# Gates and down projection of a SwiGLU MLP in three chunks of 6, 8 and 8 gates in place of four of 6, 6, 5 and 5

## The chip, the cores and the metric

The kernel runs on one core of a Trainium2 chip, in one launch. The metric is device time in microseconds (us), lower is better.

## The reference, cut to what matters

Two transformer layers over 128 context tokens and 512 latent tokens. The part that matters here is the end of each layer, the MLP, with D_MODEL = 1024 and D_FF = 2816:

```python
h2 = _rmsnorm(x, norm2_g[l]) * (1 + sc2) + sh2
a, b = jnp.split(_dwconv3(h2 @ w_up[l], ffn_conv_w[l]), 2, axis=-1)
x = x + g2 * ((jax.nn.silu(a) * b) @ w_down[l])
```

`_dwconv3` is a depthwise convolution of width 3 along the tokens. Everything is float32.

## The kernel before

**Tiling.** Tokens lie along the free dimension, T = 644 columns (640 tokens and the borders), in two halves of 322. Features lie on the 128 partitions. The 2816 hidden features are 22 gates of 128 (`N_GATE`); gate g needs a 128-column block of the a side and one of the b side of `w_up`. For float32 results each operand is split into a high part (a copy to float32r) and a low part (the difference), and every product is three matmuls: high x high, high x low, low x high. ScalarE makes the high parts of weights, VectorE the low parts.

**Gates.** Gates 0 and 6 (`CLASSIC`) are computed with plain products ahead of the loop. Each of the other 20 is computed by Strassen's scheme in seven products of 12 matmuls (128x128 by 128x322; `product`, L1185, L1187, L1189), with weights that are sums of blocks of `w_up`. SP loads seven blocks of 256 KB a gate (`up_blocks`, `block`, L565) into `raw_all`, an area of nine blocks of 512 columns; POOL makes three of the sums with adding DMAs from SBUF to SBUF (`add_block`, L678) and one with an instruction (L708). ScalarE then copies block pairs 0, 1 and 2 and last the single block A22 to `w_hi` (`up_split_hi`, L1638, L1625), and VectorE writes `w_lo` (`up_split_lo`, L2235, L2231). VectorE and ScalarE combine the seven products (L1656, L2250, L2258, L2267, L1582), apply the convolution (L1596, L2196) and silu (L1601), multiply (L2217) and split the result into `gg`, the gates' results of a chunk (L1611, L2223). `gg` holds as many gates as the largest chunk.

**Down projection.** After each chunk of gates, `down_chunk` multiplies its gates with their rows of `w_down`: 8 output tiles m, each of two token halves, each of 3 matmuls per gate (L1242, L1243, L1244) into two PSUM banks. The first two tiles leave out their last gate until it is ready. VectorE adds each tile to x (`down_add`, L2130, three pieces a tile). The weights come in four quarters of two tiles (`down_block`, L622), 256 columns a gate, alternately into slot 0 and slot 1 of `raw_all` (blocks 0 to 3 and blocks 4 to 7), and are split by L1649 and L2242. A quarter of a chunk of 5 or 6 gates is 1280 or 1536 columns, and leaves block 7 of slot 1 free.

**Order.** All queues are written out by hand, each engine's program in one order, with waits on semaphores. For the first gate of a chunk SP issues A22 (block 7) and the block for the first sum (block 8) right after the third quarter of the down weights of the chunk before; blocks 0, 2 and 3 after the third quarter's low part; blocks 4 and 5 after the fourth quarter's (`dn_lo[1]`):

```python
elif i == 0:
    sp.wait_ge(up_lo[3], n)
block(a22_block(g), 1, 1, g)
```

For the first quarter of the down weights ScalarE waits until the third product of the last gate is done. After the last layer, ten transposes of x (L820) go to PSUM banks by the list `YT_BANKS`, the first three ahead of the last down tile.

Of the kernel before, what the change touches and what calls it, by code (L numbers as in the profile page):

```python
# [8 lines left out]
F32R = mybir.dt.float32r  # L9
# [6 lines left out]
P = 128  # L16
# [13 lines left out]
T = 644  # L30
# [23 lines left out]
N_GATE = FF // P  # L54
CLASSIC = [0, 6]
N_CLASSIC = len(CLASSIC)
CHUNKS = [6, 6, 5, 5]
CH0 = [0, 6, 12, 17]
S_LAYER = N_GATE - N_CLASSIC
FIRST = 1  # L60
HELD = CLASSIC[1]
# [57 lines left out]
def chunk_of(g):  # L119

    return max(c for c in range(len(CHUNKS)) if CH0[c] <= g)


def s_gates(c):

    return [g for g in range(CH0[c], CH0[c] + CHUNKS[c]) if g not in CLASSIC]

# [14 lines left out]
def a22_block(g):  # L142

    return 7 - (g - s_gates(chunk_of(g))[0]) % 2


def s1_block(g):

    return (8, 1)[(g - s_gates(chunk_of(g))[0]) % 2]
# [5 lines left out]
def su(l, g):  # L155

    return S_LAYER * l + S_GATES.index(g)
# [15 lines left out]
def dm(l, c, m):  # L173

    return 8 * (len(CHUNKS) * l + c) + m


def dq(l, c, q):

    return 2 * (len(CHUNKS) * l + c) + q // 2  # L180

# [6 lines left out]
N_SMALL = 8  # L188
N_ROWS = 10

YT_BANKS = [6, 7, 0, 1, 3, 4, 2, 5, 6, 7]
YT_EARLY = 3
YT_WAITS = {0: 4, 2: 6, 4: 7, NT: KT}
OT_BANKS = [2, 3, 4, 0, 1]
# [17 lines left out]
def hybrid_step(nc, x_prompt, x_sample, cache_k, cache_v, c_sample, c_ctx, w_mod, b_mod, norm1_g, w_in, q_norm_g,  # L212
# [3 lines left out]
    with ctx:  # L216
        def sb(name, shape, dt=F32, scope=None):
            return (scope or ctx).enter_context(nc.sbuf_tensor(name, shape, dt))

        def sem(name):  # L220
            return ctx.enter_context(nc.semaphore(name))
# [81 lines left out]
        mlp = ExitStack()  # L303
# [18 lines left out]
        g_early = sb("g_early", [P, 2, 2, T], scope=plain)  # L322
        hfull = sb("hfull", [P, KT, T], scope=plain)
        plain.close()
        gg = sb("gg", [P, CHUNKS[0], 2, T], F32R, scope=mlp)
        mlp.close()
        ps = ctx.enter_context(nc.psum_tensor("ps", [P, 8, 512], F32))
        scores = ps[:, 2:5, :].rearrange("p b n -> p (b n)")
# [59 lines left out]
        dn_full, dn_hi, dn_lo = ([sem("%s%d" % (s, i)) for i in range(2)] for s in ("dn_full", "dn_hi", "dn_lo"))  # L388
        prod_done, gate_read = sem("prod_done"), sem("gate_read")
# [35 lines left out]
        def _(sp):  # L425
# [44 lines left out]
            for l in range(DEPTH):  # L470
                def free_of_split(n):
                    sp.wait_ge(split_full[n % 2], usable(l, n))
# [5 lines left out]
                def split_unit(n):  # L478
                    if n < C_U + 6:
                        if n < C_U:  # L480
                            load(n % 2, w_in_v, l * KT + n % 2 * KH, KH, n // 2 * QC, QC)
                        else:
                            pair, kind = divmod(n - C_U, 3)
                            col = 3 * D_ATTN + D_CONV * (1, 2, 0)[kind] + pair * UC
                            load(n % 2, w_in_v, l * KT, KT, col, UC)
                    else:
                        load(n % 2, w_out_v, l * KT, KT, (n - O_U) * UC, UC)
# [47 lines left out]
                if l:  # L535
                    sp.wait_ge(dn_lo[1], dq(l - 1, len(CHUNKS) - 1, 3) + 1)
                    split_unit(1)
# [21 lines left out]
                def free_of_slot0():  # L559

                    free_of_split(G_U)

                def block(b, row, half, g):

                    sp.dma_start(raw_f[:, BLK * b:BLK * (b + 1)].rearrange("p (t n) -> p t n", n=P),  # L565
                                 w_up_v[:, l * KT + KH * half:l * KT + KH * (half + 1),
                                        row * FF + g * P:row * FF + (g + 1) * P]).then_inc(blk_full[b], 16)

                def up_blocks(g):

                    n, c = su(l, g), chunk_of(g)
                    i = g - s_gates(c)[0]
                    if i >= 2:
                        sp.wait_ge(up_lo[3], n - 1)
                    elif c == 0:
                        free_of_split(G_U + 1)
                    elif i == 0:
                        sp.wait_ge(up_lo[3], n)
                    block(a22_block(g), 1, 1, g)
                    if i >= 2:  # L580
                        sp.wait_ge(up_lo[0], n - 1)
                        sp.wait_ge(sum_full[2], 16 * (n - 1))
                    elif i == 0 and n:
                        sp.wait_ge(up_lo[0], n)
                        sp.wait_ge(sum_full[2], 16 * n)
                    elif c == 0 and i:
                        free_of_slot0()
                    block(s1_block(g), 1, 0, g)
                    if i:
                        sp.wait_ge(up_lo[0], n)  # L590
                        sp.wait_ge(sum_full[4], 16 * n)
                    elif c == 0:
                        free_of_slot0()
                    else:
                        sp.wait_ge(dn_lo[0], dq(l, c - 1, 2) + 1)
                    block(0, 0, 0, g)
                    if i:
                        sp.wait_ge(up_lo[1], n)
                        sp.wait_ge(sum5_ready, n)
                    block(2, 0, 0, g)  # L600
                    block(3, 0, 1, g)
                    if i:
                        sp.wait_ge(up_lo[2], n)
                    elif c:
                        sp.wait_ge(dn_lo[1], dq(l, c - 1, 3) + 1)
                    block(4, 1, 0, g)
                    block(5, 0, 1, g)

                def down_block(c, q):
# [9 lines left out]
                    else:  # L619
                        sp.wait_ge(dn_lo[q % 2], dq(l, c, q - 2) + 1)  # L620
                    k0 = l * (FF // P) + CH0[c]
                    sp.dma_start(raw[:, q % 2, 0:CHUNKS[c] * DW].rearrange("p (t n) -> p t n", n=DW),  # L622
                                 w_down_v[:, k0:k0 + CHUNKS[c], q * DW:(q + 1) * DW]).then_inc(dn_full[q % 2], 16)

                for c in range(len(CHUNKS)):
                    for g in s_gates(c):
                        up_blocks(g)
                    for q in range(4):
                        down_block(c, q)
# [100 lines left out]
        def _(pe):  # L730
# [81 lines left out]
            def turn_out(j):  # L812
# [6 lines left out]
                for s in range(4):  # L819
                    ins = nc.tensor.transpose(ps[:, YT_BANKS[j], s * P:(s + 1) * P],  # L820
                                              x[:, 4 * kh + s, TOK_TILES[t]:TOK_TILES[t] + P], ident[:, :])
# [57 lines left out]
            for l in range(DEPTH):  # L879
# [353 lines left out]
                def down(c, m, k0, k1):  # L1233

                    kf, b = CHUNKS[c], m // 2 % 2
                    wh, wl = (half[:, b, 0:kf * DW].rearrange("p (t n) -> p t n", n=DW)[
                        :, :, m % 2 * P:(m % 2 + 1) * P] for half in (w_hi, w_lo))
                    for h in range(2):
                        out = ps[:, down_banks(c, m)[h], 0:HALF]
                        for k in range(k0, k1):  # L1240
                            gh, gl = (gg[:, k, i, h * HALF:(h + 1) * HALF] for i in range(2))
                            mm(out, wh[:, k, :], gh, start=k == 0, stop=False)  # L1242
                            mm(out, wh[:, k, :], gl, start=False, stop=False)  # L1243
                            ins = mm(out, wl[:, k, :], gh, start=False, stop=k == kf - 1)  # L1244
                    if k1 == kf:
                        ins.then_inc(dn_done, 1)

                def down_chunk(c):

                    kf, n = CHUNKS[c], su(l, s_gates(c)[-1])  # L1250
                    pe.wait_ge(dn_lo[0], dq(l, c, 0) + 1)
                    pe.wait_ge(g_ready, N_GATE * l + CH0[c] + kf - 1)
                    pe.wait_ge(c21_ready, n)
# [3 lines left out]
                    down(c, 1, 0, kf - 1)  # L1257
                    pe.wait_ge(g_ready, N_GATE * l + CH0[c] + kf)
                    down(c, 0, kf - 1, kf)
# [27 lines left out]
        def _(act):  # L1287
# [74 lines left out]
            for l in range(DEPTH):  # L1362
# [240 lines left out]
                def gate_hi(g):  # L1603
# [5 lines left out]
                    if g == FIRST + 1:  # L1609
                        act.wait_ge(t_ready, 4 * l + 4)  # L1610
                    A(gg[:, g - CH0[c], 0, :], gt[:, :], ACT.Copy).then_inc(gh_ready, 1)  # L1611

# [27 lines left out]
                def down_split_hi(c, q):  # L1640

                    n = su(l, s_gates(c)[-1])
                    if q < 2:
                        act.wait_ge(prod_done, 7 * n + (3, 7)[q])
                    else:
                        act.wait_ge(dn_done, dm(l, c, 2 * q - 3) + 1)
                    act.wait_ge(dn_full[q % 2], 16 * (dq(l, c, q) + 1))
                    w = CHUNKS[c] * DW
                    A(w_hi[:, q % 2, 0:w], raw[:, q % 2, 0:w], ACT.Copy).then_inc(dn_hi[q % 2], 1)  # L1649
# [17 lines left out]
                for c in range(len(CHUNKS)):  # L1667
# [31 lines left out]
                    c21(last)  # L1699
                    centre(last, 1)  # L1700
                    down_split_hi(c, 1)
                    silu(last)
                    gate_hi(last)
                    if last + 1 == HELD:
                        centre(HELD, 0)
                        centre(HELD, 1)
                    down_split_hi(c, 2)
                    if last + 1 == HELD:
                        silu(HELD)
# [18 lines left out]
            for j in range(2 * NT):  # L1728
                act.wait_ge(yT_full, j + 1)
                kh, t = divmod(j, NT)  # L1730
                A(yo[:, t, kh * 512:(kh + 1) * 512], ps[:, YT_BANKS[j], :], ACT.Copy).then_inc(yT_read, 1)

# [673 lines left out]
```

## Time and profile before

| | |
|---|---|
| median of 3 runs | 1567.98 us (1566.52 to 1570.54) |
| the profiled execution's own time | 1567.95 us |
| its span, first to last instruction | 1566.1 us |
| mean granted TensorE clock | 0.995 |
| TensorE busy | 1549.9 us, 99% |
| VectorE busy | 1046.8 us, 67% |
| ScalarE busy | 726.9 us, 46% |
| POOL busy | 188.3 us, 12% |

The page and the trace are of one execution. Busy time is the union of an engine's instructions over the span; what is outside the span lies ahead of the first instruction and behind the last. In the rows below PE is TensorE, DVE VectorE, ACT ScalarE, SP the queue that issues most DMAs; a letter q behind an engine means its sequencer. Matmuls overlap in the pipeline: one takes 310 ns and starts about 150 ns after the one before it. The MLP of layer 0 lies from about 358 to 797 us, that of layer 1 from about 1118 to 1558 us.

### The profile page before, as it was taken

The numbers are of one execution on the slowest core, as the hardware profiler recorded it, in microseconds if no ns is written. First come the engines' busy times: TensorE is split into PE (matmuls) and PEld (weight loads), VectorE is DVE, ScalarE is ACT, GpSimd is POOL, SyncE is SP. The second block draws the span as 40 slices with busy tenths as digits, with TensorE's granted clock in tenths as the row PEclk, the third lists the DMA queues.
The fourth block names the chain that finished last, engine by engine and source line by source line (L and its number), as shares of the span: only waits on it lengthen the run. The fifth ranks groups of instructions, "written<-read, shape, count | busy, mean of one in ns | idle before, by whom it ended". The sixth has DMA issues, their size and how long they took to land.

```text
span 1566.1 us, 26388 instructions
## 1 busy us (share of the span) xinstructions
PE 1549.9 (99%) x10573; PEld 1456.5 (93%) x10573; DVE 1046.8 (67%) x1661; ACT 726.9 (46%) x1218; POOL 188.3 (12%) x197
## 2 busy tenths in 40 slices
PE   8999999999999999999999999999999999999998
PEld 6778899998999999999987788899899999999998
DVE  6763767738785855858777447685688677486683
ACT  5444444326652634626454344542565355263462
POOL 1000000004202202113000000000221120130210
PEclk9999999999999999999999999999999999999999
DMA  9653011475756846659453501033367584584752
GB/s 361 244 174 136 28 54 37 156 240 138 179 142 141 199 127 160 163 146 201 155 183 127 202 28 55 28 109 108 95 145 165 137 186 132 149 192 134 181 140 85
DMA packets 278366, 225.63 MB, mean 144 GB/s; under 512 B 9674, under 2 KB 253700, under 8 KB 278244
## 3 DMA queue, kind: packets, MB, share of 16 engines
q1 hardware_dynamic: 259680, 189.89, 38.1%
q0 software_dynamic: 18320, 33.96, 12.8%
q8 instruction: 84, 1.38, 0.4%
q14 instruction: 38, 0.31, 0.1%
q10 hardware_dynamic: 244, 0.09, 0.0%
HBM read 188.78 MB, written 3.67 MB: 123 GB/s over the span
## 4 chain that ended last, share of the span: by engine, by line
PE 96%; DVE 2%; DMA 1%; ACT 1%; SPq 0%; issue 0%; DVEq 0%; ACTq 0%
PE ps L1185 11%; PE ps L1187 11%; PE ps L1189 11%; PE ps L1242 7%; PE ps L1244 7%; PE ps L1243 7%; PE ps L739 4%; PE ps L740 4%; PE ps L741 4%; PE ps L894 4%; PE ps L895 3%; PE ps L896 3%; PE ps L1034 3%; PE ps L1061 3%; PE ps L1101 3%; PE ps L1102 2%
## 5 line engine op out<-in xcount | busy, mean ns | idle before, releaser
L1638 ACT ACTIVATE w_hi<-raw_all 128x1024 fp32r<-128x1024 f32 x120 | 126.3, 1058 | 203.1 <-PE ps L1244 100.0
L1242 PE MATMUL ps<-gg,w_hi 128*128 128x322 f32 x704 | 218.5, 310 | 0.0
L1244 PE MATMUL ps<-gg,w_lo 128*128 128x322 f32 x704 | 218.2, 310 | 0.0
L1243 PE MATMUL ps<-gg,w_hi 128*128 128x322 f32 x704 | 218.1, 310 | 0.0
L1187 PE MATMUL ps<-hc_lo,w_hi 128*128 128x322 f32 x640 | 199.5, 312 | 0.0
L1185 PE MATMUL ps<-hc_hi,w_hi 128*128 128x322 f32 x640 | 199.0, 311 | 0.0
L1189 PE MATMUL ps<-hc_hi,w_lo 128*128 128x322 f32 x640 | 198.6, 310 | 0.0
L2235 DVE TENSOR_TENSOR w_lo<-raw_all,w_hi 128x1024 fp32r<-128x1024 f32 x120 | 147.7, 1230 | 72.4 <-ACT w_hi L1638 70.2
L678 POOL DMA_DIRECT2D raw_all<-raw_all x120 | 102.6, 860 | 552.6 <-DMA raw_all<-in_w_up_dram 481.0
L2196 DVE SCALAR_TENSOR_TENSOR tmp<-ub,vecs,tmp 128x642 f32<-128x642 f32 x168 | 140.9, 883 | 15.2 <-ACT tmp L1596 13.7
L2130 DVE SCALAR_TENSOR_TENSOR x<-ps,modv,x 128x128 f32<-128x128 f32 (+2 forms) x240 | 90.4, 434 | 89.8 <-PE ps L1244 54.3
L1185 PE MATMUL ps<-ht_hi,w_hi 128*128 128x322 f32 x480 | 148.8, 310 | 0.0
L1189 PE MATMUL ps<-ht_hi,w_lo 128*128 128x322 f32 x480 | 148.5, 309 | 0.0
L1187 PE MATMUL ps<-ht_lo,w_hi 128*128 128x322 f32 x480 | 148.1, 308 | 0.0
L1242 PEld LDWEIGHTS ps<-gg,w_hi 128*128 128x128 f32 x704 | 132.6, 188 | 0.0
L1244 PEld LDWEIGHTS ps<-gg,w_lo 128*128 128x128 f32 x704 | 132.6, 188 | 0.0
L1243 PEld LDWEIGHTS ps<-gg,w_hi 128*128 128x128 f32 x704 | 132.4, 188 | 0.0
L739 PE MATMUL ps<-h_hi,w_hi 128*128 128x322 f32 x384 | 123.6, 322 | 0.0
L1185 PEld LDWEIGHTS ps<-hc_hi,w_hi 128*128 128x128 f32 x640 | 120.7, 189 | 0.0
L1187 PEld LDWEIGHTS ps<-hc_lo,w_hi 128*128 128x128 f32 x640 | 120.6, 188 | 0.0
L1189 PEld LDWEIGHTS ps<-hc_hi,w_lo 128*128 128x128 f32 x640 | 120.6, 188 | 0.0
L1821 DVE TENSOR_TENSOR w_lo<-raw_all,w_hi 128x2048 fp32r<-128x2048 f32 x33 | 75.5, 2288 | 66.7 <-ACT w_hi L1346 66.7
(236 smaller groups left out, 3549.0 us busy)
## 6 DMA issues: line engine op xcount, KB each, us to landing
raw_all<-in_w_up_dram SPq DMA_DIRECT2D x280, 256.0 KB, 4.0
raw_all<-raw_all POOLq DMA_DIRECT2D x120, 256.0 KB, 3.9
raw_all<-in_w_in_dram SPq DMA_DIRECT2D x48, 512.0 KB, 6.9
mod_p<-in_w_mod_dram SPq DMA_DIRECT2D x20, 1024.0 KB, 7.3
raw_all<-in_w_down_dram SPq DMA_DIRECT2D x16, 768.0 KB, 4.4
raw_all<-in_w_down_dram SPq DMA_DIRECT2D x16, 640.0 KB, 4.1
mod_q<-in_w_mod_dram SPq DMA_DIRECT2D x8, 1024.0 KB, 9.2
raw_all<-in_w_out_dram SPq DMA_DIRECT2D x16, 512.0 KB, 4.3
```

The costliest lines, as they stand in the source:

```text
L678: pool.dma_start(raw_f[:, BLK * dst:BLK * (dst + 1)], raw_f[:, BLK * src:BLK * (src + 1)], accum_op=ALU.add).then_inc(sum_full[which], 16)
L739: mm(out, wh[:, k, col:col + P], mov_hi(k), start=k == 0, stop=False)
L1185: mm(out, whi_f[:, c0:c0 + P], hh[:, k, slot, :], start=first and k == 0, stop=False, skip_group_check=not first)
L1187: mm(out, whi_f[:, c0:c0 + P], hl[:, k, slot, :], start=False, stop=False, skip_group_check=not first)
L1189: ins = mm(out, wlo_f[:, c0:c0 + P], hh[:, k, slot, :], start=False, stop=k == KH - 1, skip_group_check=not first)
L1242: mm(out, wh[:, k, :], gh, start=k == 0, stop=False)
L1243: mm(out, wh[:, k, :], gl, start=False, stop=False)
L1244: ins = mm(out, wl[:, k, :], gh, start=False, stop=k == kf - 1)
L1638: A(whi_b[:, 2 * i:2 * (i + 1), :], src, ACT.Copy).then_inc(up_hi[i], 1)
L2130: ins = V.scalar_tensor_tensor(out=xs, in0=ps[:, banks[h], p0:p0 + n], scalar=gate, in1=xs, op0=ALU.mult, op1=ALU.add)
L2196: return V.scalar_tensor_tensor(out=cen[:, s, 1:T - 1], in0=u[:, s, j:j + T - 2], scalar=vecs[:, l, w:w + 1], in1=cen[:, s, 1:T - 1], op0= ...
L2235: V.tensor_tensor(wlo_b[:, pair, :], raw_b[:, pair, :] if i else first_pair(g), whi_b[:, pair, :].bitcast(F32), ALU.subtract).then_inc(up_ ...
```

## The change

The 22 gates of a layer are cut into chunks of 6, 8 and 8 in place of 6, 6, 5 and 5, so there are three passes of the down projection a layer in place of four. `gg` gets room for 8 gates. Quarters of the down weights of a chunk of 8 are 2048 columns and fill their slot. So the first gate of a later chunk fetches A22, and with it all that stands behind it in SP's queue, after the low part of the fourth quarter of the chunk before; and ScalarE's first copy of down weights waits for the fourth product of the last gate, since it overwrites one more block. The banks of the last transposes change with the parity of the banks of the last chunk. The room that POOL's DMAs have for descriptors is set to 2048 bytes of a partition.

```diff
@@ -54,8 +54,8 @@
 N_GATE = FF // P
 CLASSIC = [0, 6]
 N_CLASSIC = len(CLASSIC)
-CHUNKS = [6, 6, 5, 5]
-CH0 = [0, 6, 12, 17]
+CHUNKS = [6, 8, 8]
+CH0 = [0, 6, 14]
 S_LAYER = N_GATE - N_CLASSIC
 FIRST = 1
 HELD = CLASSIC[1]
@@ -188,7 +188,7 @@
 N_SMALL = 8
 N_ROWS = 10
 
-YT_BANKS = [6, 7, 0, 1, 3, 4, 2, 5, 6, 7]
+YT_BANKS = [6, 7, 3, 4, 0, 1, 2, 5, 6, 7]
 YT_EARLY = 3
 YT_WAITS = {0: 4, 2: 6, 4: 7, NT: KT}
 OT_BANKS = [2, 3, 4, 0, 1]
@@ -322,7 +322,7 @@
         g_early = sb("g_early", [P, 2, 2, T], scope=plain)
         hfull = sb("hfull", [P, KT, T], scope=plain)
         plain.close()
-        gg = sb("gg", [P, CHUNKS[0], 2, T], F32R, scope=mlp)
+        gg = sb("gg", [P, max(CHUNKS), 2, T], F32R, scope=mlp)
         mlp.close()
         ps = ctx.enter_context(nc.psum_tensor("ps", [P, 8, 512], F32))
         scores = ps[:, 2:5, :].rearrange("p b n -> p (b n)")
@@ -576,6 +576,7 @@
                         free_of_split(G_U + 1)
                     elif i == 0:
                         sp.wait_ge(up_lo[3], n)
+                        sp.wait_ge(dn_lo[1], dq(l, c - 1, 3) + 1)
                     block(a22_block(g), 1, 1, g)
                     if i >= 2:
                         sp.wait_ge(up_lo[0], n - 1)
@@ -1641,7 +1642,7 @@
 
                     n = su(l, s_gates(c)[-1])
                     if q < 2:
-                        act.wait_ge(prod_done, 7 * n + (3, 7)[q])
+                        act.wait_ge(prod_done, 7 * n + (4, 7)[q])
                     else:
                         act.wait_ge(dn_done, dm(l, c, 2 * q - 3) + 1)
                     act.wait_ge(dn_full[q % 2], 16 * (dq(l, c, q) + 1))
@@ -2391,7 +2392,8 @@
     import concourse.bacc as _bacc
     from concourse.bass_utils import run_bass_kernel_spmd as _run
 
-    nc = _bacc.Bacc("TRN2", target_bir_lowering=False, num_devices=1)
+    nc = _bacc.Bacc("TRN2", target_bir_lowering=False, num_devices=1,
+                     dynamic_dma_scratch_size=2048)
     tables = _tables()
     arrays, args = {}, []
     for name in _INS + ["ident", "rope"]:
```

## Rows read from the trace of the kernel before

Each group is of the one profiled execution.

**Rows 1.** The page: busy time of the engines, the chain, costly groups

```profile
PE 1549.9 (99%) x10573; PEld 1456.5 (93%) x10573; DVE 1046.8 (67%) x1661; ACT 726.9 (46%) x1218; POOL 188.3 (12%) x197
...
PE 96%; DVE 2%; DMA 1%; ACT 1%; SPq 0%; issue 0%; DVEq 0%; ACTq 0%
...
L1242 PE MATMUL ps<-gg,w_hi 128*128 128x322 f32 x704 | 218.5, 310 | 0.0
...
L2130 DVE SCALAR_TENSOR_TENSOR x<-ps,modv,x 128x128 f32<-128x128 f32 (+2 forms) x240 | 90.4, 434 | 89.8 <-PE ps L1244 54.3
...
L1821 DVE TENSOR_TENSOR w_lo<-raw_all,w_hi 128x2048 fp32r<-128x2048 f32 x33 | 75.5, 2288 | 66.7 <-ACT w_hi L1346 66.7
```

**Rows 2.** Waits of TensorE: waited for, us in total, times, longest

```profile
PE ps L1159 <- DVE hc_lo L2179: 3.1, 2, 2.0
...
PE ps L894 <- DVE h_lo L1909: 0.3, 1, 0.3
```

**Rows 3.** Busy time by stretch: four gates, down chunks of 6 and 5

```profile
391.90:441.80 49.90, 49.90 (x340) 49.90 (x339) 40.07 (x50) 34.31 (x51) 14.16 (x14) 1.00 0.75 176
454.20:496.80 42.60, 42.60 (x290) 42.60 (x289) 24.00 (x37) 11.43 (x13) 5.59 (x6) 1.00 0.55 141
...
663.70:699.20 35.50, 35.50 (x243) 35.50 (x242) 19.25 (x32) 8.49 (x9) 5.55 (x6) 1.00 0.58 155
```

**Rows 4.** TensorE in order of time, both ends of a down chunk

```profile
454.07 0.31 PE L1189 MATMUL ps<-hc_hi,w_lo 128*128 128x322 f32 x1
454.22 0.31 PE L1242 MATMUL ps<-gg,w_hi 128*128 128x322 f32 x1
...
496.80 0.31 PE L1185 MATMUL ps<-hc_hi,w_hi 128*128 128x322 f32 x1
```

**Rows 5.** ScalarE, then VectorE in order of time, ahead of that chunk

```profile
448.28 1.48 ACT L1649 ACTIVATE w_hi<-raw_all 128x1536 fp32r<-128x1536 f32 x1
...
449.10 0.49 DVE L2250 TENSOR_TENSOR ub<-ps,s 128x322 f32<-128x322 f32 x1 [1.63 <-PE ps L1189]
...
451.27 1.75 DVE L2242 TENSOR_TENSOR w_lo<-raw_all,w_hi 128x1536 fp32r<-128x1536 f32 x1
```

**Rows 6.** ScalarE's groups by form

```profile
L1346 ACT ACTIVATE w_hi<-raw_all 128x2048 fp32r<-128x2048 f32 x35 | 66.9, 1913 | 8.6 <-PE ps L896 8.6
```

**Rows 7.** SP, VectorE, POOL in order of time, during that chunk

```profile
440.79 22.13 SPq L622 DMA_DIRECT2D raw_all<-in_w_down_dram  x4
462.96 57.37 SPq L565 DMA_DIRECT2D raw_all<-in_w_up_dram  x25
...
479.02 2.02 SPq L565 DMA_DIRECT2D raw_all<-in_w_up_dram  x4
...
477.23 1.76 DVE L2242 TENSOR_TENSOR w_lo<-raw_all,w_hi 128x1536 fp32r<-128x1536 f32 x1 [4.25 <-ACT w_hi L1649]
...
482.37 0.84 POOL L678 DMA_DIRECT2D raw_all<-raw_all  x1 [6.32 <-DMA raw_all<-in_w_up_dram]
```

**Rows 8.** ScalarE, then VectorE in order of time, for gate 8

```profile
504.11 1.06 ACT L1638 ACTIVATE w_hi<-raw_all 128x1024 fp32r<-128x1024 f32 x1 [0.71 <-PE ps L1189]
...
506.29 1.22 DVE L2235 TENSOR_TENSOR w_lo<-raw_all,w_hi 128x1024 fp32r<-128x1024 f32 x1
```

**Rows 9.** DMAs issued at L565, L678 and L622, in this order

```profile
DMA to landing us min/median/max: 2.7/4.0/6.8
...
DMA to landing us min/median/max: 3.1/3.9/6.9
...
DMA to landing us min/median/max: 4.0/4.3/5.6
```

**Rows 10.** What L1185 waited for; ScalarE in order of time before it

```profile
  ACT s L1656: 0.3, 1
...
1189.76 1.06 ACT L1638 ACTIVATE w_hi<-raw_all 128x1024 fp32r<-128x1024 f32 x1 [3.12 <-DMA raw_all<-raw_all]
```

**Rows 11.** POOL in order of time, around its 113th DMA

```profile
1350.95 0.86 POOL L678 DMA_DIRECT2D raw_all<-raw_all  x1 [1.17 <-DMA raw_all<-in_w_up_dram]
```

## The prediction

> **What bounds the kernel now.** I read first the page's busy shares and its chain. TensorE is busy 1549.9 of 1566.1 us and holds 96% of the chain that ended last [rows 1]. A busy share can still hide stalls, so I read next TensorE's own waits: ten entries, 12 us together, the longest 3.1 us before the MLP's first matmuls, and none at a line of the gates or the down projection [rows 2]; only the view of L1185 by itself shows one of 0.3 us there [rows 10]. Third, the stretches that the change touches. TensorE is busy in every one of the 49.90 us of four gates and of the 42.60 and 35.50 us of a down chunk of 6 and one of 5, at a granted clock of 1.00 [rows 3]. Fourth, the seams: from gates to down projection one matmul starts 0.15 us after the other, as everywhere else, and at the way back, 496.80, the busy stretch of 42.60 us ends without a hole [rows 3, 4]. So the seams that the change takes away (one each way in each layer, four in all) cost TensorE nothing today.
>
> **TensorE's sum.** The down projection has the same matmuls: 22 gates x 8 tiles x 2 halves x 3 x 2 layers = 2112, which is 3 x 704 [rows 1]. A chunk of 6 takes 42.60 us, so 5.33 us for each of its 8 tiles; one of 5 takes 35.5, 4.44 a tile [rows 3]. One of 8 should take 42.60 x 8/6 = 56.8, 7.10 a tile. Per layer that is 2 x 42.6 + 2 x 35.5 = 156.2 us before and 42.6 + 2 x 56.8 = 156.2 after. The gates' 40 x 84 matmuls stay as well. TensorE's term is 0, and what is left is whether one of its waits turns up.
>
> **What is removed.** One pass a layer that adds the down result to x: 8 tiles x 3 pieces x 2 layers = 48 of VectorE's instructions at 434 ns [rows 1], 20.8 us. They lie beside TensorE's gapless stream, so they are worth 0 on the path. And the rows of gates grow, from 5 at most to 7 and 8. If the fetching fell behind a little with every gate, a longer row would run dry. But ScalarE's copy for gate 8 at 504.11 was released by TensorE, after 0.71 us of idling, and not by a DMA [rows 8]: TensorE paces the row, which has nothing to lose with length. Term 0.
>
> **The first down weights** are 128x2048 for a chunk of 8, and ScalarE's copy (L1649) waits for the fourth product of the last gate, not the third. VectorE's instruction behind the fourth product (L2250) starts at 449.10, so ScalarE may start there instead of at 448.28 [rows 5]. A copy of 128x2048 takes 1.91 us [rows 6], to 451.01. VectorE's half (L2242) began at 451.27, held by its own queue, since ScalarE had been done at 449.76 [rows 5]. So its start stays. It grows from 1.75 to 2.29 us [rows 1, 5] and ends at 453.56, where the first down matmul is due at 454.22 [rows 4]. The margin falls from 1.20 to 0.66 us: term 0. Were it x late beyond that, it would cost x four times (two chunks of 8, two layers). The load, 1 MB instead of 768 KB, was issued at 440.79 [rows 7] and has 8.3 us to 449.10; these loads land in 4.0 to 5.6 us [rows 9].
> Queued behind L2242 on VectorE is L2267, 0.54 us later; ScalarE's centre tap, the silu and the last gate's product wait for it. That product is needed after two tiles less their last gate, 2 x 7/8 x 7.10 = 12.4 us into the chunk, where a chunk of 5 gave 2 x 4/5 x 4.44 = 7.1 us. The second weights are due after 14.2 us instead of 8.9, and all later ones have 14.2 us for copies of 1.91 + 2.29. So only the first weights are tight; the rest of the down projection is looser than before.
>
> **The late A22 block.** SP issued the next gate's first two blocks at 462.96, right behind the third down load, and its last blocks at 479.02, behind VectorE's half of the fourth down weights (477.23 + 1.76 = 478.99) [rows 7]. Now the first one waits for that too. SP's queue has this gate's six other blocks behind the wait, and two of the gate that follows; all nine go in one burst. Waiting for them are POOL's adding DMAs and its own sum, then ScalarE's copies, then VectorE's halves. I count the seam after the chunk of 6 from 478.99. A load lands in L and an adding DMA in A; POOL takes 0.5 between a landing and the next issue, an estimate from the 3.35 us between the loads at 479.02 and the DMA at 482.37, which L's shortest 2.7 nearly fills [rows 7, 9]; ScalarE copies 1.06, VectorE 1.22 [rows 8], and 0.2 (an estimate) goes in handing over. With the medians L = 4.0 and A = 3.9 [rows 9] the first pair is ready at 478.99 + 4.0 + 0.5 + 3.9 + 0.2 + 2.3 = 489.9; it is due at 496.80 [rows 4]. The second pair has one adding DMA more, 489.9 + 0.5 + 3.9 = 494.3, and is due two products later: 12 matmuls at 0.148 us (49.90 us over 4 x 84) are 1.78, so 500.4. Margins of 6.9 and 6.1 us. For the gate after, POOL's own sum of some 2 us comes first, and the adding DMAs land near 498.3 and 502.8, ahead of the 504.11 at which its second pair is copied now [rows 8]. Term 0. After a chunk of 8 the fourth weights are ready 4 x 7.10 + 0.2 + 1.91 + 2.29 = 32.8 us in, and the gates are due at 56.8: 24 us instead of 17.8, looser still.
> The bound from the other side takes the longest landings of the trace, L = 6.8 and A = 6.9 [rows 9]: first pair 495.7, in time; second 503.1, late by 2.7 us, in each of two layers: 5.4 us. I take 0, because all three would have to be at their longest in one chain. That a late adding DMA can reach TensorE is seen once: ScalarE waited 3.12 us for one until 1189.76, and TensorE lost 0.3 us [rows 10].
>
> **Less room for descriptors.** POOL's DMAs get 2048 bytes of a partition. No row shows a room that is short. From below the cost is nothing: in a gate POOL mostly waits for landings, so two or three are under way. From above it is priced as rival B. I take nothing, since POOL's issues take 0.84 to 0.86 us early and late [rows 7, 11].
> The Trainium skill (DMA: Bandwidth & Descriptors, Terms and The descriptor swizzle) has 16 bytes for a descriptor, and 8 plus one for completion on each engine for 128 partitions; its page SBUF — State Buffer (SBUF size: 192, 224, or 256?) has 16 KiB as the usual room. By these figures the ring goes round every 113 of POOL's DMAs before and every 14 now. The trace must then show one turn, near 1351 us, and the issue there takes 0.86 us [rows 11]: by that rule a turn is free and the sum stays.
>
> **The sum** of all terms is 0 on the profiled execution's 1567.95 us (1566.1 of span, 1.85 around it); the runs' median is 1567.98. Predicted: 1568.0 us.
>
> **The rivals.** A, slower by the late A22 block, at the seam after the chunk of 6. For it: nine loads share one start, and landings of 6.8 and 6.9 us occur. Against it: 6.1 us of margin. It costs from the point where L + 2A exceeds its median of 11.8 us by 6.1; at the longest, 1568.0 + 5.4 = 1573.4 us. Chance 0.05.
> B, slower by the room: two adding DMAs stand ahead of a gate's second pair. For gate 8 VectorE is done with it at 506.29 + 1.22 = 507.5 [rows 8], due at 496.80 + 12.45 + 3.56 = 512.8. So 5.3 us, 2.65 for each DMA, are hidden. At 3 us each it costs 0.7 us in each of 40 gates: 1596 us. Against it: [rows 11]. Chance 0.02.
> C, faster, if the seams or the 48 adds cost something after all. All that the records leave is the 0.3 us of [rows 10], which gives 1567.7; beyond 4.7 us, a quarter of the adds' 20.8 us would have to lie on the path, 1562.8. Chance 0.04.
> D, the change does nothing but what it is written to do, which is the forecast.
>
> **Chances and range.** Within 0.3%, 4.7 us, about what a measurement of this kernel can tell from no change: 0.88. Slower 0.08: A 0.05, B 0.02, late first weights 0.01. Faster 0.04. The range reaches from 1564.5, most of the way to C's outer price, to A's bound of 1573.4.
>
> **What would show it.** TensorE's count and busy time stay, L1242 is still x704 at 310 ns, the adds of L2130 are x192 instead of x240, and a down chunk of 8 is busy in all of 56.8 us. The first L2242 of such a chunk ends 0.6 to 0.7 us ahead of the first down matmul. After the chunk of 6, nine loads go in one burst and VectorE's first half is ready some 7 us ahead of its product. The prediction is wrong if TensorE waits for more than a microsecond at a product or at L1242, or if POOL's issue takes visibly more than 0.86 us.

## The result, and the profile after

| | before | after |
|---|---|---|
| median of 5 runs | 1568.88 us (1566.52 to 1570.54) | 1574.75 us (1573.61 to 1577.76) |
| ratio to before, 95% interval | | 1.0042 [1.0031, 1.0053] |
| span of the profiled execution | 1566.1 us | 1572.9 us |
| mean granted TensorE clock | 0.995 | 0.995 |

The change costs 5.9 us by the medians and 6.6 by the means, which the ratio compares. The forecast was no change, 1568.0 us, and the median lies 1.35 us above its range.

The page of the kernel after: busy time of the engines, then two of its costly groups (busy, mean ns of one | idle time before, and what ended most of it).

```profile
PE 1554.5 (99%) x10573; PEld 1457.7 (93%) x10573; DVE 1020.6 (65%) x1605; ACT 724.1 (46%) x1210; POOL 185.0 (12%) x197
...
L1639 ACT ACTIVATE w_hi<-raw_all 128x1024 fp32r<-128x1024 f32 x120 | 126.9, 1058 | 208.5 <-DMA raw_all<-raw_all 119.4
L2131 DVE SCALAR_TENSOR_TENSOR x<-ps,modv,x 128x128 f32<-128x128 f32 (+2 forms) x192 | 72.3, 433 | 108.5 <-PE ps L1245 74.5
...
L1186 PE MATMUL ps<-ht_hi,w_hi 128*128 128x322 f32 x480 | 149.7, 312 | 4.4 <-ACT s L1657 4.2
```

TensorE has the same 10573 matmuls, VectorE has lost the 48 adds, and a wait has come that [rows 2] don't have: TensorE at L1186, a product's first matmul, for ScalarE's `s` (L1657). (The `s` is ScalarE's copy of a gate's first product out of PSUM; I call it the snapshot.) The second sign is upstream: ScalarE idled 119.4 us ahead of L1639 for adding DMAs. The waits of the kernel after: who waited, for what, us in total, times, the longest.

```profile
PE ps L1186 <- ACT s L1657: 4.2, 7, 1.0
...
ACT w_hi L1639 <- DMA raw_all<-raw_all: 119.4, 45, 14.2
```

Before, the same ScalarE wait was 20.6 us in 14 waits. (Lines behind the added wait are one higher after: L1638 of before is L1639.)

Where the time went I took from the starts of matmuls. From the start of the first Strassen product of a layer to that of its last down matmul it takes 404.57 us in layer 0 and 406.17 in layer 1 before, 405.71 and 411.88 after: 6.85 us more, where the whole span has grown by 6.8. Between the starts of a product's last matmul and the next one's first lie 0.15 us; where more lies there I call the rest a stall. The stalls add up to 0.2 us before and 6.0 after, and all but 0.1 us of these stand ahead of the third product of a gate (0.64 and 0.18 us in layer 0; 1.13, 1.01, 0.34, 0.37, 0.89, 0.29 and 0.99 in layer 1, and one of 0.02). Of them 1.79 us are in chunk 0, 4.07 in the rows of 8. The matmul behind a stall is 0.1 us longer too (0.41 us below in place of 0.31), which makes up most of what is missing to 6.85.

TensorE in order of time at the stall of gate 9 in layer 1, whose first product starts at 1284.16 (start, duration, what; in brackets the idle time and what ended it):

```profile
1287.56 0.31 PE L1190 MATMUL ps<-ht_hi,w_lo 128*128 128x322 f32 x1
1288.72 0.41 PE L1186 MATMUL ps<-ht_hi,w_hi 128*128 128x322 f32 x1 [0.85 <-ACT s L1657]
1288.98 0.31 PE L1188 MATMUL ps<-ht_lo,w_hi 128*128 128x322 f32 x1
```

ScalarE in order of time at that gate, and then at gate 16, which has no stall and whose first product starts at 1431.1:

```profile
1285.32 1.06 ACT L1639 ACTIVATE w_hi<-raw_all 128x1024 fp32r<-128x1024 f32 x1 [3.18 <-DMA raw_all<-raw_all]
1286.29 0.82 ACT L1597 ACTIVATE tmp<-ub,vecs 128x644 f32<-128x644 f32 x1
1287.01 0.42 ACT L1583 ACTIVATE ub<-ps 128x322 f32<-128x322 f32 x1
1287.51 0.83 ACT L1597 ACTIVATE tmp<-ub,vecs 128x644 f32<-128x644 f32 x1
1288.25 0.42 ACT L1657 ACTIVATE s<-ps 128x322 f32<-128x322 f32 x1
...
1429.52 1.06 ACT L1639 ACTIVATE w_hi<-raw_all 128x1024 fp32r<-128x1024 f32 x1 [2.47 <-PE ps L1190]
1430.48 0.82 ACT L1597 ACTIVATE tmp<-ub,vecs 128x644 f32<-128x644 f32 x1
1431.31 0.44 ACT L1583 ACTIVATE ub<-ps 128x322 f32<-128x322 f32 x1
1432.12 0.83 ACT L1597 ACTIVATE tmp<-ub,vecs 128x644 f32<-128x644 f32 x1 [0.38 <-ACT ub L1583]
1433.11 0.44 ACT L1657 ACTIVATE s<-ps 128x322 f32<-128x322 f32 x1
```

The same two places before, at gate 9 of layer 1, whose first product starts there at 1282.03: POOL's third adding DMA, and ScalarE's copy of the third pair, which waits for TensorE.

```profile
1273.71 0.85 POOL L678 DMA_DIRECT2D raw_all<-raw_all  x1 [1.10 <-DMA raw_all<-in_w_up_dram]
...
1280.44 1.06 ACT L1638 ACTIVATE w_hi<-raw_all 128x1024 fp32r<-128x1024 f32 x1 [2.47 <-PE ps L1189]
```

This is the chain that I had not drawn. L1639 is here the copy of the gate's third pair (blocks 4 and 5); the third adding DMA of a gate is the one that adds block 0 to block 4. That pair is not needed until the fifth product: in gate 16 it has 1.06 us of copy and 1.22 of VectorE to go from 1429.52 and is due at 1431.1 + 4 x 1.78 = 1438.2, 6.4 us later. But ScalarE's queue has four more instructions behind it, and the fourth of these, the snapshot of the first product, is what TensorE needs ahead of its third. Packed, the snapshot starts 1288.25 - 1285.32 = 2.93 us after the copy. It takes 0.42 and is due 2 x 1.78 = 3.56 us into the gate. So the copy may start at +0.2 us, and in gate 16 it started at 1429.52 - 1431.1 = -1.6. The margin of the third adding DMA is some 1.8 us, not 6.4. In gate 9 the copy started at +1.16, 1.0 us too late, and TensorE lost 1.01 us.

POOL in order of time ahead of that, in the kernel after:

```profile
1278.13 0.87 POOL L679 DMA_DIRECT2D raw_all<-raw_all  x1 [0.51 <-DMA raw_all<-in_w_up_dram]
```

This is gate 9's third adding DMA, issued 6.0 us ahead of the gate (8.3 before); it took 7.1 us to land. The lines of L679 and of the loads at L565 after, from issue to landing:

```profile
DMA to landing us min/median/max: 3.2/4.2/7.1
...
DMA to landing us min/median/max: 2.7/4.4/7.4
```

In [rows 9] they were 3.1/3.9/6.9 and 2.7/4.0/6.8. So the longest were already there, and the kernel before stood them.

What changed is the lead. The three adding DMAs for the first gate behind the chunk of 6 are issued 27.6, 21.6 and 14.4 us ahead of it before, and 13.6, 7.3 and 6.7 us after (layer 1: 12.6, 6.8, 6.2). The second adding DMAs of gates 8 to 11 of layer 0 go 14.8, 9.5, 9.2 and 8.6 us ahead of their gates before, and 9.0, 8.3, 8.0 and 7.4 after. In both kernels this lead, once it is under 10 us, shrinks in most steps from gate to gate (by up to 2.5 us), and where it grows without a stall of TensorE it is by 0.3 us at most: a buffer comes free, a load, a sum and another sum follow, and that ring takes about the 12.4 us that TensorE needs for a gate. A chunk that starts without a lead runs at the edge sooner, and then a long landing goes through to TensorE.

The landings themselves grow too. In gates 7 to 11 of both layers the third adding DMA lands in 3.95 us on average before and in 5.26 after. So the late start takes from both sides: the DMA goes later and takes longer. Why it takes longer no run separates; with the lead given back (run 3) it is 4.55, with the late start alone (run 1) 4.68.

### The profile page after: what moved, and what is told of

Same layout as the page of the kernel before. It is cut to its first block and busy times, and to the rows that moved or that the text cites. A ratio compares the mean times of both kernels' runs of the same rounds, so it can differ in the third digit from the quotient of the medians.

```text
span 1572.9 us, 26304 instructions
## 1 busy us (share of the span) xinstructions
PE 1554.5 (99%) x10573; PEld 1457.7 (93%) x10573; DVE 1020.6 (65%) x1605; ACT 724.1 (46%) x1210; POOL 185.0 (12%) x197
## 5 line engine op out<-in xcount | busy, mean ns | idle before, releaser
L1639 ACT ACTIVATE w_hi<-raw_all 128x1024 fp32r<-128x1024 f32 x120 | 126.9, 1058 | 208.5 <-DMA raw_all<-raw_all 119.4
L1186 PE MATMUL ps<-hc_hi,w_hi 128*128 128x322 f32 x640 | 199.1, 311 | 0.0
L679 POOL DMA_DIRECT2D raw_all<-raw_all x120 | 103.0, 869 | 495.4 <-DMA raw_all<-in_w_up_dram 458.2
L1186 PE MATMUL ps<-ht_hi,w_hi 128*128 128x322 f32 x480 | 149.7, 312 | 4.4 <-ACT s L1657 4.2
L2131 DVE SCALAR_TENSOR_TENSOR x<-ps,modv,x 128x128 f32<-128x128 f32 (+2 forms) x192 | 72.3, 433 | 108.5 <-PE ps L1245 74.5
L1186 PEld LDWEIGHTS ps<-hc_hi,w_hi 128*128 128x128 f32 x640 | 120.7, 189 | 0.3 <-DVE ub L2259 0.3
L741 PE MATMUL ps<-h_lo,w_hi 128*128 128x322 f32 x384 | 119.7, 312 | 0.0
```

Of the source, the lines that this page charges most:

```text
L679: pool.dma_start(raw_f[:, BLK * dst:BLK * (dst + 1)], raw_f[:, BLK * src:BLK * (src + 1)], accum_op=ALU.add).then_inc(sum_full[which], 16)
L741: mm(out, wh[:, k, col:col + P], mov_lo(k), start=False, stop=False)
L1186: mm(out, whi_f[:, c0:c0 + P], hh[:, k, slot, :], start=first and k == 0, stop=False, skip_group_check=not first)
L1639: A(whi_b[:, 2 * i:2 * (i + 1), :], src, ACT.Copy).then_inc(up_hi[i], 1)
```

## The experiments

Each kernel is compared with the kernel before on its own chip. Theory T: the late start of A22 takes the lead, and the third adding DMA delays the snapshot. Rivals: the smaller room for descriptors; the length of the rows by itself. "Product waits" are TensorE's waits at the first matmul of a product for ScalarE's `s`, as in the view of the waits.

**1. The late wait alone, in the kernel before.**

```diff
                         sp.wait_ge(up_lo[3], n)
+                        sp.wait_ge(dn_lo[1], dq(l, c - 1, 3) + 1)
```

> Theory 1 (the lead): the late A22 block takes away the lead of POOL's adding DMAs over a row of gates; the third sum then lands so late that ScalarE's copy of the third pair holds up the snapshot queued behind it, and TensorE waits at L1185. The kernel before with the late A22 wait alone, in its chunks of 6, 6, 5 and 5, has six seams without a lead in rows of 5 gates: 2 to 5 us slower than before, 1570 to 1574, stalls at L1185 in the later rows. Theory 2 (the room): the smaller room for descriptors, or the shifted SBUF addresses that come with it, makes landings longer; this kernel keeps the old room, so 1568 to 1569.

Measured 1578.43 us, 1.0056 [1.0043, 1.0069]. The waits of TensorE in its trace:

```profile
PE ps L1186 <- ACT s L1657: 5.8, 5, 2.6
```

That is above the 1570 to 1574 expected. One added wait gives a loss of the size of the whole one (the intervals overlap), by the same kind of stall. But the seams aren't those of the kernel after. The worst stalls, 1.37 us in layer 0 and 2.74 in layer 1, are in the second gate behind a chunk of 5, which has the shortest down projection to catch up in; by the starts of matmuls all of the loss in this trace is behind the chunks of 5 or in chunk 0, and none in the rows of 5 gates behind the chunks of 6. So this run shows that a late start can do it, not what it costs in the kernel after. POOL and ScalarE at the stall in layer 0:

```profile
708.71 0.85 POOL L679 DMA_DIRECT2D raw_all<-raw_all  x1 [1.19 <-DMA raw_all<-in_w_up_dram]
...
714.02 1.06 ACT L1639 ACTIVATE w_hi<-raw_all 128x1024 fp32r<-128x1024 f32 x1 [0.56 <-DMA raw_all<-raw_all]
...
717.19 0.42 ACT L1657 ACTIVATE s<-ps 128x322 f32<-128x322 f32 x1
```

The same chain: third adding DMA, copy, and the snapshot 3.17 us behind it. (Its profiled execution, 1573.51 us, is the fastest of its five.)

**2. The smaller room alone, in the kernel before.**

```diff
-    nc = _bacc.Bacc("TRN2", target_bir_lowering=False, num_devices=1)
+    nc = _bacc.Bacc("TRN2", target_bir_lowering=False, num_devices=1,
+                     dynamic_dma_scratch_size=2048)
```

> The kernel before with the room for descriptors of the changed kernel (2048 bytes) and nothing else. Theory 1: no change, 1568 to 1569, median landing of the adding DMAs 3.9 us as before. Theory 2: the whole loss or most of it, 1572 to 1575, median landing 4.2 us or more in all rows.

Measured 1568.65 us, 1.0002 [0.9993, 1.0010]. The room costs nothing that can be told; the adding DMAs land in 4.0 us (median; 3.9 before).

**3. The kernel after with its lead given back.** A tenth block takes the first A22 of a chunk, so the added wait goes. (The 2 KB a partition are free.)

```diff
 def a22_block(g):
-    return 7 - (g - s_gates(chunk_of(g))[0]) % 2
+    i = g - s_gates(chunk_of(g))[0]
+    return 7 - i % 2 if i else 9
...
-        raw_all = sb("raw_all", [P, 9 * BLK])
+        raw_all = sb("raw_all", [P, 10 * BLK])
...
-                        sp.wait_ge(dn_lo[1], dq(l, c - 1, 3) + 1)
```

> The changed kernel with a tenth block in raw_all for the A22 of each chunk's first gate, so that it is fetched early again, in chunks of 6, 8 and 8 with the small room. Theory 1: the lead is back, and what remains is the length of the rows, 0 to 2 us: 1568 to 1571, first adding DMA of a row 23 us or more ahead of its gate. Theory 2: the loss stays, 1573 to 1576. A third theory, that rows of 7 and 8 gates run dry by themselves whatever the lead: 1572 to 1575 with stalls only from the sixth gate of a row on.

Measured 1571.35 us, 1.0015 [1.0006, 1.0024]. The waits of TensorE:

```profile
PE ps L1186 <- ACT s L1657: 1.9, 3, 1.0
```

The lead is worth (1.0042 - 1.0015) x 1568.7 = 4.2 us of the 6.6 by the same ratios; with the intervals of the two, from 2 to 6.5. What stays, 2.4 us, is in gates that nothing delays at the seam. By the starts of matmuls 1.20 and 0.38 us are lost at gates 18 and 19 of layer 1, the fifth and sixth of a row of 8, and 1.0 in chunk 0. That the length of the rows costs something by itself is likely, and not shown: the 1.6 us are of one row in one execution, they start at a fifth gate, which the kernel before has too, and the same row of layer 0 loses nothing.

**4. The kernel after with a larger room,** 6080 bytes, `dynamic_dma_scratch_size=6080` in place of 2048.

> The changed kernel with 6080 bytes of room for descriptors instead of 2048. Theory 1: no change to the changed kernel, 1573 to 1576. Theory 2, if it is the size of the room: part of the loss goes, 1568 to 1572; if it is the shift of addresses: anything up to 5 us either way of the changed kernel.

Measured 1583.80 us, 1.0103 [1.0088, 1.0119], with 9.7 us of product waits in 12. Neither theory had this: with more room the kernel is slower, by 9 to 10 us against after. It is taken up in runs 7, 8 and 11.

**5. The third sum by POOL, in the kernel after.** The second test of T, from the other end: the late start stays, but the third adding DMA (5 to 7 us from issue to landing where it hurts) becomes an instruction of POOL.

```diff
-                    add_block(4, 0, 4)
+                    b0, b4 = (raw_f[:, b * BLK:(b + 1) * BLK] for b in (0, 4))
+                    nc.gpsimd.tensor_tensor(b4, b4, b0, ALU.add).then_inc(sum_full[4], 16)
```

> The changed kernel with the third sum of each gate (block 4 += block 0) as an instruction on POOL, as the fourth one is, instead of an adding DMA. Theory 1a: TensorE waits only because the landing of the third adding DMA (5 to 7 us) holds ScalarE's copy of the third pair, and with it the snapshot queued behind; an instruction of 1.5 to 2 us ends that: stalls at L1185 below 1 us in all, time 1567 to 1569.5. Theory 1b: the whole chain of loads and adding DMAs runs late and the third sum is only where it shows; the second sum would then do the same: stalls of 2 us and more stay, 1571 to 1575. Rival: POOL's instructions slow VectorE or the chain, 1575 or more.

Measured 1566.58 us, 0.9989 [0.9979, 0.9999]. The view of stretches, layer 0 from 385 to 782 us (length, then busy time and count of TensorE, its weight loads, VectorE, ScalarE and POOL, the granted clock, DMA share, GB/s), and the durations of the new instruction (ns, min/median/max):

```profile
385.00:782.00 397.00, 397.00 (x2686) 397.00 (x2685) 292.73 (x357) 194.16 (x268) 94.42 (x75) 1.00 0.59 157
...
L1640 ACT ACTIVATE w_hi<-raw_all 128x1024 fp32r<-128x1024 f32 x120 | 127.1, 1059 | 181.0 <-PE ps L1191 76.6
...
L706 POOL TENSOR_TENSOR raw_all<-raw_all x40: 1287/1608/3222, 374.3 to 1477.5; 128x512 f32<-128x512 f32 x40
```

TensorE is busy in all of 397 us, and for more than half of the time that ScalarE's copies wait they wait for TensorE again. A sum of 1.6 us (3.2 at the longest) in place of one of 4.2 (7.1) takes the whole loss away, though A22 starts late and the rows are long. So the loss goes through the third adding DMA, as the traces of the stalls show. What this run doesn't separate is its length from what it does to others: with it gone the loads land in 3.6 us in place of 4.4 (medians) and the two other adding DMAs in 3.9 in place of 4.2 and 4.1. Nor is it free: VectorE's halves of the pairs (L2237 here) take 1.42 us in the mean in place of 1.25.

**6. The late wait only behind a chunk of 8.** A chunk of 6 leaves block 7 free, so its successor may start early.

```diff
-                        sp.wait_ge(dn_lo[1], dq(l, c - 1, 3) + 1)
+                        if CHUNKS[c - 1] == 8:
+                            sp.wait_ge(dn_lo[1], dq(l, c - 1, 3) + 1)
```

> The changed kernel with the A22 wait only at the seam after a chunk of 8, where the block is really overwritten; after the chunk of 6 it is fetched early as before. Theory 1 (a late start costs its row): the row of gates 7 to 13 gets its lead back, the row of 14 to 21 stays as it is, 1570 to 1573. If only the length of the rows mattered, no change: 1573 to 1576.

Measured 1570.21 us, 1.0016 [1.0007, 1.0025], product waits 1.5 us in 3 (and 0.8 in 2 ahead of fifth products). As good as run 3: the seam behind the chunk of 6 is the one that costs, and behind a chunk of 8 a late start costs nothing that can be told. (The profiled execution is the slowest of its runs, 1573.61 us, at a granted clock of 0.993.)

**7 and 8. Two other rooms, in the kernel after:** 5888 and 2176 bytes. They came out of looking for what run 4 had changed. The room lies ahead of `raw_all` in a partition: by the compiled programs `raw_all` starts at byte 22784 = 89 x 256 after (145 x 256 before), and at 26816 = 104 x 256 + 192 in run 4. 5888 bytes put it at 104 x 256, 2176 at 89 x 256 + 128.

> The changed kernel with 5888 bytes of room. 6080 bytes gave 1583.8, which neither theory expected. If that came from where the blocks start (6080 shifts them by 64 bytes against a grid of 256, 5888 keeps the changed kernel's place on that grid), this one takes 1573 to 1576, landings of the adding DMAs at a median of 4.2. If a larger room itself slows POOL's DMAs, 1582 to 1585.

> The changed kernel with 2176 bytes of room, which puts the start of raw_all on a multiple of 256 bytes (it stands 128 beside one in both kernels, by the order of allocation). If the place on that grid sets the landings, they are shorter than the changed kernel's (loads below 4.4, adding DMAs below 4.2 us) and stalls shrink: 1568 to 1573. If the place has no part in it, 1573 to 1576.

(The second text has the two kinds of place the wrong way round; the one of run 11 puts it right.) Measured 1574.08 us, 1.0036 [1.0024, 1.0049] with 5888 bytes, like after; and 1582.40 us, 1.0094 [1.0080, 1.0108] with 2176, like run 4. So not the size: a large room and a small one are both cheap on the grid of 256 bytes and both dear off it.

**9 and 10. The third sum by POOL with the tenth block of run 3, and in the kernel before.**

> Both repairs on the changed kernel: the tenth block, so that A22 is fetched early at every seam, and the third sum as an instruction on POOL. With all waits of the gates gone, the chunks of 6, 8 and 8 have nothing left but TensorE's stream: 1565 to 1568, like the kernel with the third sum on POOL alone (1566.6). If the early block still gives something beside it, 1564 to 1566.

> The kernel before, chunks of 6, 6, 5 and 5, with the third sum as an instruction on POOL. If the gain of the third sum on POOL over the kernel before (0.9989) is the sum's own and owes nothing to the larger chunks, this takes the same 1566 to 1567.5. If the larger chunks contribute, it stays at 1568 to 1569.

Measured 1566.88 us, 0.9984 [0.9975, 0.9993], and 1567.49 us, 0.9991 [0.9982, 1.0000]. TensorE has no product waits in run 9. The three kernels with this sum are alike, with chunks of 6, 8 and 8 or without. So without the stalls the change of the chunks is worth nothing that can be told, which is what "TensorE's sum" and "What is removed" said of it: four seams fewer and 48 adds fewer buy no time. Run 9 is 0.16% ahead of before, but not apart from run 5 or run 10, and for run 10, the sum by POOL in the kernel before, the interval reaches 1.0000.

**11. A shift of 128 bytes with the room left at 2048,** by a spare 32 columns ahead of the first buffer that is not the room.

```diff
+        sb("shift", [P, 32])
```

> The changed kernel, room 2048, with 128 unused bytes ahead of x, so that raw_all stands where it stood with a room of 2176 bytes. In the compiled programs raw_all starts at 22784 = 89 x 256 in the changed kernel, at 37120 = 145 x 256 in the kernel before, and 128 and 192 beside a multiple of 256 with rooms of 2176 and 6080, the two slow ones; so the expectation of the run with 2176 had the two places the wrong way round. If the place on the grid of 256 bytes makes the loss, this takes 1580 to 1585; if the size of the room does, 1573 to 1576.

Measured 1580.67 us, 1.0072 [1.0059, 1.0084], 8.3 us of product waits in 8. That settles it between the two: the place, not the room. Which buffer's place it is, this run leaves open, since it shifts all of them; ScalarE's copies keep their 1058 ns in the mean and VectorE's halves 1.25 us, so it isn't the reading by these engines. The adding DMAs and the loads (L680 and L566 here), from issue to landing:

```profile
DMA to landing us min/median/max: 3.2/4.4/6.5
...
DMA to landing us min/median/max: 2.9/4.6/6.8
```

The medians are 0.2 us longer than after (0.3 and 0.4 in run 4). The shortest landing of an adding DMA is 3.24 or 3.25 us in the three kernels off the grid, and 3.13 to 3.16 in the eleven others. That is little, but a gate's second pair has a load and two of these in its chain, and the ring is already as long as a gate.

**12. Only A22 late, in the kernel after.** The block for the first sum and blocks 0, 2 and 3 are issued early again; A22 alone waits for the fourth quarter.

```diff
-                        sp.wait_ge(dn_lo[1], dq(l, c - 1, 3) + 1)
-                    block(a22_block(g), 1, 1, g)
+                    late = c > 0 and i == 0
+                    if not late:
+                        block(a22_block(g), 1, 1, g)
...
+                    if late:
+                        block(a22_block(g), 1, 1, g)
```

> The changed kernel with only the A22 block itself behind the fourth quarter: the block for the first sum goes early, blocks 0, 2 and 3 after the third quarter as before, A22 then with blocks 4 and 5. Theory: what costs is the lead of the first adding DMA, which still needs A22, so little comes back: 1572 to 1575. Rival: what costs is the burst of nine loads in SP's queue behind the wait; three to four loads leave it, so 1569 to 1571.

Measured 1573.25 us, 1.0029 [1.0019, 1.0040], product waits 4.5 us in 7. It lies halfway between after (1.0042) and run 3 (1.0015), within the noise of either half. So the wait for A22 itself keeps about half of what the lead is worth: the first sum needs A22, the second needs the first, and POOL takes the sums in order. The other half may be the other blocks of the burst; these intervals don't separate it from nothing.

## Why the prediction was wrong

**What held.** The matmuls and the adds are those of "TensorE's sum" and "What is removed". The view of stretches for the first down chunk of 8, and for three stalled gates:

```profile
585.30:641.90 56.60, 56.60 (x385) 56.60 (x385) 21.91 (x32) 10.93 (x10) 5.56 (x6) 1.00 0.41 112
...
1284.20:1321.50 37.30, 36.06 (x240) 35.26 (x240) 28.76 (x37) 23.40 (x36) 10.89 (x12) 1.00 0.89 202
```

56.6 us, where 56.8 were forecast, and TensorE is busy in all of them: the seams are without a hole. "The first down weights": VectorE's half and the first down matmul, in order of time:

```profile
582.33 2.28 DVE L2243 TENSOR_TENSOR w_lo<-raw_all,w_hi 128x2048 fp32r<-128x2048 f32 x1
...
585.27 0.31 PE L1243 MATMUL ps<-gg,w_hi 128*128 128x322 f32 x1
```

582.33 + 2.28 = 584.61, 0.66 us ahead of 585.27: the forecast 0.66. "Less room for descriptors": POOL's issues at L679 take 869 ns in the mean for 860, and run 2 measures no cost (rival B falls). Its place for the turn near 1351 us counted every DMA of POOL as one of 128 partitions, which eight of the first ten are not, so the turn would come later. The reading stands: from the 109th DMA to the last no issue before takes longer than 0.88 us.

The first seam of "The late A22 block" held as well. SP and then VectorE, in order of time:

```profile
480.03 5.91 SPq L565 DMA_DIRECT2D raw_all<-in_w_up_dram  x9
...
491.34 1.23 DVE L2236 TENSOR_TENSOR w_lo<-raw_all,w_hi 128x1024 fp32r<-128x1024 f32 x1 [8.19 <-ACT w_hi L1639]
```

The nine loads go in one burst, and the first pair is ready at 492.57 and due at 497.8. That is 5.2 us of margin for the forecast 6.9; the first adding DMA took 5.9 us to land in place of 3.9. No stall stands at this gate or, in layer 0, at the next three. But gate 8's second adding DMA landed at 506.43, where 502.8 was forecast: the medians of the kernel before were too short for this row.

**The step that failed** is that the wait for the fetched and summed blocks was put at 0 in two terms: in "The late A22 block", and at the end of "What is removed": "TensorE paces the row, which has nothing to lose with length. Term 0." The second rests on one row, ScalarE's copy for gate 8 [rows 8], of a gate that had the lead of the early A22 behind it. The pace was read from a row of gates with a lead, and the lead is what the change takes away. Runs 3 and 5 measure it: 4.2 us (2 to 6.5) by the lost lead, up to 2.4 by the length and by chunk 0, and nothing of either when POOL makes the third sum.

"The late A22 block", the larger of the two, failed in two ways. It followed the first two pairs of the first two gates, each to its own product, and took the lateness for over when these had margins. It left out the third pair; that one's own product is due latest. But in a queue that runs in order an instruction must be done before the first thing behind it that somebody needs: for the third copy that is the snapshot, 1.8 us away, not the fifth product, 6.4 us away. And it stopped after the second gate; the stalls come in the third gate and later of the row. With the third adding DMA issued 6 us ahead of its gate, a landing of 6.2 us uses up the margin, and [rows 9] had landings up to 6.9; at the nine stalls it was issued 4.9 to 6.0 us ahead and took 5.3 to 7.1 us. One such row stood among those read: the wait of 3.12 us that made 0.3 us of stall at gate 4 of layer 1 [rows 10]. I cited it as a case seen once, while chunk 0 is the chunk that has the least lead already in the kernel before: its third adding DMAs go 4.9 to 6.5 us ahead of its third to fifth gates there, those of the other rows 5.8 to 8.3.

**Rival A** had the right cause and side, at 0.05. Its place (the second pair of the first gate), its condition (three landings at their longest in one chain) and its size (2 x 2.7) are not what happened: nine stalls of 0.2 to 1.1 us, in later gates, nearly all from one long landing of the third adding DMA (at gate 17 of layer 1 the second was late, landing in 5.8 us). "What would show it" did name the sign, a wait at a product of over a microsecond: 1.0 and 1.13 us at the longest.

**What stays open.** Chunk 0, whose schedule the change doesn't touch, has 1.79 us of the stalls after and 0.2 before; in run 3 it has 1.0, in run 5 0.15. It runs at the edge in all of them. Chance in the landings of one execution may be part of it, but the traces fall in two groups: with the third sum by DMA and the buffers on the grid of 256 bytes, chunk 0 loses 0.2, 0.4 and 1.0 us in the three kernels of 6, 6, 5 and 5 (before, runs 2 and 1), and 1.0, 1.1, 1.8, 2.0 and 2.5 in the five of 6, 8 and 8 (runs 3 and 7, after, runs 6 and 12). So some 1 us of the loss may come from something else in the change, such as the larger `gg` and the places of the buffers; no run tests it, and theory T doesn't explain it. Nor is it settled where the 0.1% of runs 5, 9 and 10 against before comes from. From the first Strassen product to the last down matmul their two layers take together 0.1 us more, 0.4 less and 0.1 less than before, so what their profiled spans are shorter by (2.3, 1.7 and 0.4 us) lies mostly outside, where they do the same work as before.

## What to carry to other kernels

Measure the margin of an instruction to the first thing that anybody needs behind it in its own queue, not to the use of its own result. Before a start is made later, ask what lead the steps behind it live on, and whether the loop of buffer, load and sums is shorter than the engine's pace; if it is not, lateness is hardly made up, and the place to look for the cost is some iterations on. A gapless engine at one iteration says who sets the pace there, with the lead it has there.

## What the hardware showed that was not expected

The place of the buffers in their SBUF partition matters, by 5 to 10 us in this kernel, and the landings of the DMAs at `raw_all` go with it. With `raw_all` at 89 x 256 or 104 x 256 bytes: 1.0042 and 1.0036. At 128 bytes off that grid: 1.0094 and 1.0072; at 192 off: 1.0103. The median landing of the adding DMAs goes from 4.2 to 4.4 and 4.5 us with it, that of the 256 KB loads from 4.4 to 4.6, 4.7 and 4.8. The Trainium skill (DMA: Bandwidth & Descriptors, How a descriptor splits into AXI transactions) says that a read transaction must start at a 256-byte boundary, so that a descriptor off it fetches bytes that it doesn't use. The direction agrees with these landings; it is told there of reads, and the loads only write to this buffer, so that part no run here explains. Whoever changes the size of anything that lies ahead of such a buffer changes two things at once.

The lengths of SBUF-to-SBUF adding DMAs and of the same sum on POOL lie far apart in this kernel: 256 KB in 3.2 to 7.1 us (median 4.2, after) by DMA with 0.87 us of POOL for its issue, 1.3 to 3.2 us (median 1.6, run 5) as POOL's instruction.
